# Two layers of a 1024-wide model on one core: gate logits in split form, scores of both directions summed, and token halves behind the second layer's output projection

## The reference, cut to what matters

```python
def gla_chunked(q, k, v, logg):          # one direction; the other one runs on flipped tokens
    b = jnp.cumsum(logg, axis=3)
    qe = q * jnp.exp(b)
    ke = k * jnp.exp(-b)
    a = jnp.where(mask, jnp.einsum('bhncd,bhnjd->bhncj', qe, ke), 0.0)
    o_intra = jnp.einsum('bhncj,bhnjv->bhncv', a, v)
    ...
    o = o_intra + jnp.einsum('bhncd,bhndv->bhncv', qe, s_before)

def gla_mixer(h, w_in, w_gate_up, b_gate, out_g, w_o):
    ...
    logit = jnp.einsum('bsir,ire->bsie', z, w_gate_up.astype(f32)) + b_gate.astype(f32)
    ...
    o = rmsnorm(o_f + o_b, out_g).reshape(B, S, GLA_V)

def second_block(...):
    y = _hybrid_mixer(h, w_in, ..., w_out, cos, sin)         # ends in merged @ w_out
    x = x + g1 * _rmsnorm(y, norm_g[l, 1])
    h = _rmsnorm(x, norm_g[l, 2]) * (1.0 + sc2) + sh2
    y = _conv_ffn(h, w_up, conv_w, conv_b, w_down)
    x = x + g2 * _rmsnorm(y, norm_g[l, 3])
```

## Time and profile before

| what | value |
| --- | --- |
| time, median of 3 runs | 2041.51 us (2040.54 to 2043.55) |
| profiled execution | 2038.21 us, its span 2036.5 us |
| mean granted TensorE clock | 0.989 of full |
| TensorE busy | 1990.7 us, 98% |
| VectorE, ScalarE, GpSimd busy | 1126.3, 745.3, 575.2 us |
| linear attention, heads (us from start) | 765 to 817 |
| layer two, last `w_out` matmul to first feed-forward matmul | 1632.6 to 1655.8 |

### The profile page before, as it was taken

One profiled execution on the slowest core, in us unless ns is written; L12 is line 12 of the kernel. 1 busy time (PEld: TensorE's weight loads), 2 busy tenths in 40 slices (PEclk: granted clock), 3 DMA queues, 4 the chain that ended last, 5 costly groups with the idle time before them and its releaser, 6 DMA issues.

```text
span 2036.5 us, 23938 instructions
## 1 busy us (share of the span) xinstructions
PE 1990.7 (98%) x9414; PEld 1625.2 (80%) x9414; DVE 1126.3 (55%) x1132; ACT 745.3 (37%) x801; POOL 575.2 (28%) x513
## 2 busy tenths in 40 slices
PE   9999999999999999999999999999999979999996
PEld 7766788888877988888888877788888858888885
DVE  6797355555564437455465456773334465545446
ACT  6665332322334523332222234345552343222322
POOL 1101289993000000189993002522310100000000
PEclk9999999999999999999999999999999999999998
DMA  7300144442222220144442213412123312332231
GB/s 227 98 21 1 62 170 151 154 165 97 88 67 103 84 101 23 62 157 155 163 158 92 100 62 130 114 42 84 63 83 110 104 56 84 103 103 102 83 103 42
DMA packets 32781, 202.01 MB, mean 99 GB/s; under 512 B 3872, under 2 KB 4000, under 8 KB 10048
## 3 DMA queue, kind: packets, MB, share of 16 engines
q1 hardware_dynamic: 25984, 168.44, 24.1%
q0 software_dynamic: 6720, 32.51, 5.1%
HBM read 191.50 MB, written 2.10 MB: 95 GB/s over the span
## 4 chain that ended last, share of the span: by engine, by line
PE 93%; DVE 4%; ACT 2%; issue 1%; DMA 0%; SPq 0%; DVEq 0%; ACTq 0%
PE ps L260 26%; PE ps L262 26%; PE ps L261 25%; PE ps L700 2%; PE ps L1609 1%; PE ps L687 1%; PE ps L382 1%; PE ps L290 1%; PE ps L292 1%; PE ps L291 1%; PE ps L1156 1%; PE ps L1593 1%; PE ps L676 1%; PE ps L675 1%; PE ps L1164 1%
## 5 line engine op out<-in xcount | busy, mean ns | idle before, releaser
L222 ACT ACTIVATE w_hi<-w_raw 128x2048 fp32r<-128x2048 f32 x143 | 274.0, 1916 | 676.8 <-PE ps L262 676.6
L230 DVE TENSOR_TENSOR w_lo<-w_raw,w_hi 128x2048 fp32r<-128x2048 f32 x139 | 323.3, 2326 | 158.5 <-ACT w_hi L222 156.9
L260 PE MATMUL ps<-h_hi,w_hi 128*128 128x512 f32 x944 | 380.4, 403 | 10.7 <-DVE h_lo L440 5.4
L262 PE MATMUL ps<-h_hi,w_lo 128*128 128x512 f32 x944 | 372.5, 395 | 0.0
L261 PE MATMUL ps<-h_lo,w_hi 128*128 128x512 f32 x944 | 372.2, 394 | 0.0
L392 POOL TENSOR_TENSOR sq<-sq 128x1024 f32<-128x1024 f32 x11 | 36.4, 3307 | 825.9 <-ACT sq L361 705.9
L1405 POOL TENSOR_SCALAR ada_t<-ada_w,prm 128x256 f32<-128x256 f32 x192 | 220.3, 1147 | 13.3 <-DMA ada_w<-in_ada 12.4
L260 PEld LDWEIGHTS ps<-h_hi,w_hi 128*128 128x128 f32 x944 | 180.0, 191 | 55.1 <-issue 13.6
L262 PEld LDWEIGHTS ps<-h_hi,w_lo 128*128 128x128 f32 x944 | 179.9, 191 | 38.4
L261 PEld LDWEIGHTS ps<-h_lo,w_hi 128*128 128x128 f32 x944 | 180.4, 191 | 36.5 <-issue 1.2
L1013 DVE TENSOR_TENSOR x<-x,ps 128x1024 f32<-128x1024 f32 x128 | 155.8, 1217 | 80.8 <-PE ps L262 80.8
(11 more groups left out here) (312 smaller groups left out, 3211.4 us busy)
## 6 DMA issues: line engine op xcount, KB each, us to landing
w_raw<-in_wb SPq DMA_DIRECT2D x153, 1024.0 KB, 4.9
ada_w<-in_ada POOLq DMA_DIRECT2D x24, 1024.0 KB, 5.3
a_sw<-a_g POOLq DMA_DIRECT2D x20, 128.0 KB, 2.7
x<-in_xT SPq DMA_DIRECT2D x4, 512.0 KB, 7.8
out_T<-x SPq DMA_DIRECT2D x4, 512.0 KB, 2.8
x_rot<-x_g POOLq DMA_DIRECT2D x12, 128.0 KB, 3.0
w_raw<-in_wb SPq DMA_DIRECT2D x4, 256.0 KB, 6.4
b_k<-b_k POOLq DMA_DIRECT2D x4, 256.0 KB, 5.3
```

The costliest lines, as they stand in the source:

```text
L222: act.activation(w_hi[:, slot], w_raw[:, slot], ACT.Copy).then_inc(hi_done, 1)
L230: dve.tensor_tensor(w_lo[:, slot], w_raw[:, slot], w_hi[:, slot].bitcast(F32), ALU.subtract).then_inc(split_done, 1)
L260: pe.matmul(out, w[0], h[0], start=start, stop=False)
L262: return pe.matmul(out, w[1], h[0], start=False, stop=stop)
```

## The change

1. Gate logits. The z block holds z three times (rows 0 to 31, 32 to 63, 64 to 95). `g_z` becomes fp32r over 128 rows: high part, low rest, high part. The gate weights come in a 128-row table (512 KB instead of 128) and are stacked as high, high, low rest. Each head's product is then one fp32r matmul. VectorE gets three instructions (`gate_parts`).
2. Scores. A new VectorE instruction `both_ways` adds the masked scores of both directions, and TensorE multiplies the sum by the values: half the matmuls of line 1156. `sums(h - 1)` moves ahead of the chunk products. The decays of the keys of heads 1 to 3 move from VectorE (2 instructions of 512 columns) to ScalarE (8 of 128 columns); those of head 1 come during the projections.
3. Layer two. The last `w_out` block and both blocks of the first feed-forward unit are done in two token halves of 256 columns; norm, addition, second norm and split run by halves, one half's vector work beside the other's matmuls. `y` isn't cleared any more. The last `w_out` rows are read from PSUM. Squares of `x` are summed by 256-column ones-matmuls, those of half 1 between the tiles of block 1 of half 0.
4. Semaphores of four table loads are joined in one (`tables_in`), norms are renumbered.

```diff
 def logits(d):
     if d == 0:
-        pe.wait_ge(gup_in, 16)
-        pe.wait_ge(g_ev, 1)
+        pe.wait_ge(g_zl, 1)
     ...
-        last = pe.matmul(ps[:, 4 + h, :], gl["g_up"][:, d, h * P:(h + 1) * P], gl["g_z"][:], start=True, stop=True)
+        last = pe.matmul(ps[:, 4 + h, :], gl["g_ups"][:, d, h * P:(h + 1) * P], gl["g_z"][:], start=True, stop=True)
 for h in range(GLA_H):
+    if h >= 1:
+        sums(h - 1)
     pe.wait_ge(g_kc, 2 * h + 2)
     ...
-    if h >= 1:
-        sums(h - 1)
-    pe.wait_ge(g_am, 2 * (h + 1))
+    pe.wait_ge(g_as, h + 1)
     ...
-            for d in range(2):
-                pe.matmul(ps[:, bank + i, t * P:(t + 1) * P], gl["g_v"][:, t, vcol], gl["g_a"][:, d, t, :],
-                          start=t == 0 and d == 0, stop=False)
+            pe.matmul(ps[:, bank + i, t * P:(t + 1) * P], gl["g_v"][:, t, vcol], gl["g_a"][:, 0, t, :],
+                      start=t == 0, stop=False)
```

The parts on VectorE and ScalarE, and layer two on TensorE:

```diff
+def gate_parts():                                   # VectorE, ahead of the projections
+    up, whole = gl["g_ups"], gl["g_up"]
+    dve.wait_ge(gup_in, 16)
+    link(dve, dve.tensor_copy(up[:], whole[:]))
+    dve.tensor_tensor(up[64:96], whole[64:96], up[64:96].bitcast(F32), ALU.subtract)
+    dve.wait_ge(g_ev, 1)
+    dve.tensor_tensor(gl["g_z"][32:64], ps[32:64, 0, :], gl["g_z"][32:64].bitcast(F32), ALU.subtract).then_inc(g_zl, 1)
+def both_ways(h):                                   # VectorE, behind queries(h)
+    dve.wait_ge(g_am, 2 * (h + 1))
+    dve.tensor_tensor(a[:, 0], a[:, 0], a[:, 1], ALU.add).then_inc(g_as, 1)
+def decayed(h):                                     # ScalarE, behind rstd of head h - 2
+    for d in range(2):
+        for n in range(TT):
+            ins = act.activation(gl["g_kd"][:, d, w], qk("g_k", d)[:, h, w], ACT.Copy, scale=...)
+        ins.then_inc(g_kd, 1)
...
+def wout_pe(pe, b0):
+    pe_block(pe, b0, b0 % 2, hh, 3, each=lambda k: pe.wait_ge(t_lo, k // 2 + 1))
+    pe_block(pe, b0 + 1, (b0 + 1) % 2, hh, 1)
+    pe_block(pe, b0 + 2, b0 % 2, hh, 0)
+    pe.wait_ge(split_done, b0 + 4)
+    pe.wait_ge(proj_ev, 10)
+    half(0, b0 + 3, lambda k: None).then_inc(o_part, 1)
+    half(1, b0 + 3, first_sums).then_inc(block_done, 1)      # first_sums: at k == 3, waits o_fold 3 and o_sq 4
+    pe.wait_ge(o_sq, 5)
+    half_sums(1)
 def ffn_pe(pe, b0, n):
-    ffn_up(pe, 0, b0, b0 % 2, rows=56)
+    for j in range(4):
+        renorm_sums(pe, 0, j)
+    ffn_up_half(pe, b0, 0, 0)                                # waits r_lo tile by tile
+    ffn_up_half(pe, b0, 1, 0, each=lambda k: renorm_sums(pe, 1, k - 1) if k in (1, 2, 3, 4) else None)
+    ffn_up_half(pe, b0, 0, 1)
+    ffn_up_half(pe, b0, 1, 1)
...
+def wout_act(act, b0):
+    ...                                                      # squares of y, half 0 of the last rows
+    std(0, o_sum, 1)
+    act.wait_ge(block_done, b0 + 4)
+    act.activation(quarter_slot(1), half_rows(1), ACT.Square).then_inc(o_sq, 1)
+    ...                                                      # four quarters of the next high part between square(0, 0..3)
+    std(1, o_sum, 2)
+    std(0, r_sum, 4)
+    rows(0)
+    for j in range(4):
+        square(1, j)
+    std(1, r_sum, 8)
+    rows(1)
+def wout_dve(dve, b0):
+    ...                                                      # three copies to y, each with the rest of a block
+    added(0)
+    split_lo(dve, b0 + 5, (b0 + 5) % 2)
+    rows(0)
+    added(1)
+    rows(1)
+def wout_pool(pool):                                         # two folds of 1024 columns and one of 512
```

More of the change, by code:

```diff
@@ L1228, in gla_act @@
                     turned(0)
+                    decayed(1)
             act.preload_act_table_set("natural_log_exp_and_others")
@@ L1370, in gla_dve @@
                     queries(h + 1)
+                    both_ways(h + 1)
             root(GLA_H - 1)
@@ new lines, in build, with quarter_slot, renorm_slot, half_sums @@
+        std_count = lambda which, h: 6 + 2 * which + h + 1
+        HALF_BANK = (2, 4)
+        half_rows = lambda h: ps[:, HALF_BANK[h]:HALF_BANK[h] + 2, HALF[h]]
+        def quarter_slot(i):
+            return ff["f_c"][:, i // 2, (i % 2) * S:(i % 2 + 1) * S].rearrange("p (a s) -> p a s", a=2)
+        def renorm_slot(q):
+            return quarter_slot((2, 3, 0, 1)[q % 4])
+        def wout_pe(pe, b0):
+            hh = (mx["x_mhi"], mx["x_mlo"])
+            def half_sums(h):
+                for i in range(2):
+                    last = pe.matmul(ps[:, 6 + h, 0:S // 2], ones[:], quarter_slot(h)[:, i, :], start=False, stop=i == 1)
+                last.then_inc(o_sum, 1)
+            def half(h, b, each):
+                for k in range(KT):
+                    each(k)
+                    for n in range(2):
+                        last = three(pe, ps[:, HALF_BANK[h] + n, HALF[h]], wtile(b % 2, k * 256 + n * P),
+                                     (hh[0][:, k, HALF[h]], hh[1][:, k, HALF[h]]), k == 0, k == KT - 1)
+                return last
+            def first_sums(k):
+                if k == 3:
+                    pe.wait_ge(o_fold, 3)
+                    for h in range(2):
+                        pe.matmul(ps[:, 6 + h, 0:S // 2], ones[:], sq[:, 0, HALF[h]], start=True, stop=False)
+                    pe.wait_ge(o_sq, 4)
+                    half_sums(0)
+            pe_block(pe, b0, b0 % 2, hh, 3, each=lambda k: pe.wait_ge(t_lo, k // 2 + 1))
[7 more added lines that the diff above has]
+            half_sums(1)
@@ new lines, in renorm_sums, with std, square, rows @@
+        def renorm_sums(pe, h, j):
+            pe.wait_ge(r_sq, 4 * h + j + 1)
+            for i in range(2):
+                last = pe.matmul(ps[:, 6 + h, 0:S // 2], ones[:], renorm_slot(4 * h + j)[:, i, :],
+                                 start=j == 0 and i == 0, stop=j == 3 and i == 1)
+            last.then_inc(r_sum, 1)
+        def wout_act(act, b0):
+            def std(h, needed, count):
+                act.wait_ge(needed, count)
+                alink(act, act.activation(rstd[:, HALF[h]], ps[:, 6 + h, 0:S // 2], ACT.Ln, bias=pc("eps"), scale=1.0 / D))
+                act.activation(rstd[:, HALF[h]], rstd[:, HALF[h]], ACT.Exp, scale=-0.5).then_inc(n_std, 1)
+            def square(h, j):
+                q = 4 * h + j
+                act.wait_ge(o_add, q + 1)
+                if q == 3:
+                    act.wait_ge(o_sum, 2)
+                elif q >= 4:
+                    act.wait_ge(r_sum, q - 3)
+                act.activation(renorm_slot(q), x[:, 2 * j:2 * j + 2, HALF[h]], ACT.Square).then_inc(r_sq, 1)
+            def rows(h):
+                for k in range(KT):
+                    act.wait_ge(n_row, 16 + 8 * h + k + 1)
+                    act.activation(h_hi[:, k, HALF[h]], trow[:, k % 4, HALF[h]], ACT.Identity,
+                                   bias=modT[:, 24 + k:25 + k]).then_inc(n_hi, 1)
+            act.wait_ge(n_app, 48)
+            for j in range(2):
+                next_hi(act, b0 + j + 2, (b0 + j) % 2)
+                act.wait_ge(proj_ev, 8 + j + 1)
+                act.activation(two(sq[:, j]), y[:, 2 * j:2 * j + 2, :], ACT.Square).then_inc(o_sq, 1)
+            next_hi(act, b0 + 4, b0 % 2)
+            act.wait_ge(proj_ev, 11)
+            act.wait_ge(o_fold, 1)
+            act.activation(two(sq[:, 1]), y[:, 4:6, :], ACT.Square).then_inc(o_sq, 1)
+            act.wait_ge(o_part, 1)
+            act.activation(quarter_slot(0), half_rows(0), ACT.Square).then_inc(o_sq, 1)
+            std(0, o_sum, 1)
+            act.wait_ge(block_done, b0 + 4)
+            act.activation(quarter_slot(1), half_rows(1), ACT.Square).then_inc(o_sq, 1)
+            b = b0 + 5
+            quarter_hi(act, b, b % 2, 0)
+            square(0, 0)
+            quarter_hi(act, b, b % 2, 1)
+            quarter_hi(act, b, b % 2, 2)
+            square(0, 1)
+            quarter_hi(act, b, b % 2, 3)
+            square(0, 2)
+            square(0, 3)
+            std(1, o_sum, 2)
[5 more added lines that the diff above has]
+            rows(1)
@@ new lines, in ffn_up_half @@
+        def ffn_up_half(pe, b, which, h, each=None):
+            pe.wait_ge(split_done, b + which + 1)
+            for k in range(KT):
+                if which == 0:
+                    pe.wait_ge(r_lo, 8 * h + k + 1)
+                if each is not None:
+                    each(k)
+                for n in range(2):
+                    last = three(pe, ps[:, 2 * which + n, HALF[h]], wtile((b + which) % 2, k * 256 + n * P),
+                                 (h_hi[:, k, HALF[h]], h_lo[:, k, HALF[h]]), k == 0, k == KT - 1)
+            if h == 1:
+                last.then_inc(block_done, 1)
@@ L2570 @@
     i = {k: np.asarray(v) for k, v in inputs.items()}
-    up = zeros(32, 2, S)
-    up[0:16, 0] = i["gla_w_gate_up"][0, 0]
-    up[16:32, 1] = i["gla_w_gate_up"][0, 1]
+    up = zeros(P, 2, S)
+    for r in range(0, 96, 32):
+        up[r:r + 16, 0] = i["gla_w_gate_up"][0, 0]
```

(1 more changed line is left out.)

180 lines of the change are left out of this document (110 added, 70 removed).

## The result

The changed kernel takes 2018.64 us (median of 4 runs, 2015.13 to 2020.76) beside 2042.32 (4 runs, 2040.54 to 2043.55): ratio 0.989 (0.9874 to 0.9905). A second measurement of it, beside eleven runs of the kernel before, gave 0.9903 (0.9887 to 0.9919). Its profiled execution took 2016.82 us, with a span of 2015.0 and a mean granted clock of 0.991. The forecast was 2020.8, within 2016.5 to 2028.

The account below looks back on a forecast made before the run. TensorE, in flight for 98% of the span, was taken as the bound. Gains of 7.4 (logits), 9.0 (heads) and 4.3 (layer two) sum to 20.7 us, taking the median from 2041.5 to 2020.8, range 2016.5 to 2028.

Parts of the forecast that it names:

- Logits: Gate logits: fp32r products save 5.4 us, no clock fall 1.7, small steps between matmul types the rest; 7.4 in all.
- The wait before block 8: TensorE's wait of about 1 us for block 8's rest on VectorE was to shift with its chain and not grow.
- Heads: Linear attention heads: a turn of 11.8 us instead of 14.17 three times, and 1.9 in head 0; gain 9.0 us.
- I charge 0.2: Heads: the first state is ready 0.1 to 0.3 us after TensorE is, so 0.2 us of waiting per turn.
- at most 0.3 ahead of the scores: Sign for the heads: TensorE would stand at most 0.3 us ahead of scores times values.
- The rival of a bound VectorE: Heads: VectorE, done at 12.6 with next scores at 12.65, becomes the bound; 2024 to 2028 us, chance 0.12.
- This works only since the decays of keys left VectorE: Heads: VectorE is just in time only because the key decays, 2 x 0.69 us, moved to ScalarE.
- Layer two: From `w_out` to the third feed-forward block: token halves overlap vector work with matmuls; gain 4.3 us after latency.
- The price of 0.39 for a product of 256 columns: Layer two, VectorE's `added`: a 256-column product was taken as 0.39 us, between 0.33 and 0.48.
- 12 us from the last `w_out` matmul to the first of the feed-forward part: Sign for layer two: the gap between these two matmuls would be 12 us, with sums between them.
- steps 1 and 3: Layer two's rebuilt schedule: half 1 of the last `w_out` block ends at 1635.3; TensorE starts feed-forward at 1644.6.
- Slow clock in the heads: Rival: the clock falls to 1.2 GHz in the heads, costing 40 us; time 2061 us, chance 0.03.

Follow-up runs that it names:

- the double and the padded sets: Kernel before with each fp32 gate-logits product made twice (logits stage 148.91 us against 135.44), or made over 128 rows, the added ones zero (133.13 and 133.11).
- l2_only: Kernel before with layer two's token halves alone, logits and heads as before; 2034.37 us (8 runs), ratio 0.997.
- decays_dve: Changed kernel with the decays of the keys back on VectorE as two instructions of 512 columns; 2019.23 us (4 runs), ratio 0.9894.
- whole_second: Changed kernel with the sums of half 1 at once, then half 1 of block 0, then block 1 whole; layer two took 67.10 us, 3.3 more.

## Why the prediction was right, point by point

- **Logits, 7.4 expected, 7.4 measured**, and nearly with the split that was given: 5.4 by the step of the matmuls, 0.4 by the small step behind each set (0.3 was added for it), 1.6 by the clock (1.7 expected). That the logits bring the fall was a guess from what stood ahead of it, and the double and the padded sets bear it out. That it cost 1.7 and not twice that was the luck of this execution, as `l2_only` shows. The wait before block 8 stayed at 1.1 us and moved with its chain.
- **Heads, 9.0 expected, 8.0 measured.** Head 0 gave 1.8 of its 1.9. A turn came out at 12.09 instead of 11.75. Step for step: `within` 2.66 (2.65), sums 1.72, first chunks 1.31 (1.35), second chunks and wait 1.70 (1.35 + 0.2), scores times values 2.02 (1.8), queries times states 2.68. The step that failed is "I charge 0.2" for the states: the wait itself is 0.36, and the matmuls behind it lose 0.24. Together with small differences of the other terms that makes the turn 0.34 longer, three times. Right was that a wait for the states takes over; wrong the signs to look for, "at most 0.3 ahead of the scores".
- **The rival of a bound VectorE** (2024 to 2028) put its price on work that came 0.05 us before its date. The date was the wrong one: VectorE is done at 12.65, as reckoned, but had 1.2 us of its own idle time behind that date and 0.4 ahead of it, and `decays_dve` spent 1.1 of these without any cost. "This works only since the decays of keys left VectorE" was wrong.
- **Layer two, 4.3 expected, 4.6 measured** in this pair of traces, 5.7 on the average. With the 16.9 us by which this part lies earlier after the change, the steps compare at once: first feed-forward matmul 1644.7 (predicted 1644.6), half 0 of block 1 done 1661.4 (1661.5), half 1 of block 0 done 1667.6 (1667.7), rest of the weights awaited 1.36 (1.3), third block done 1685.8 (1685.7). The price of 0.39 for a product of 256 columns, taken between 0.33 and 0.48, is 0.40 in the chain. The 0.3 taken off for latency was too much. What the sum never says is that the 34.6 us of before from which it starts hold 1.7 us of low clock behind the stand at 1655.84: 1.3 of the 4.6 are the clock and not the overlap that the prediction tells of. One sign was written wrongly: it named 12 us from the last `w_out` matmul to the first of the feed-forward part, where steps 1 and 3 themselves give 9.3, and 9.3 it is.
- **Slow clock in the heads**: 1.00 over the whole turn, so nothing of it.
- **The median.** 2020.8 was forecast, and 2018.64 and 2020.54 were measured. The stages say that the change is worth 7.9 + 8.0 + 5.7 = 21.6 us, with the logits and layer two averaged over the traces. The two series gave 23.7 and 18.8, one on each side of it. That the first median lay 2.2 from the forecast is within that chance and no merit of the sum: the heads gave 1.0 less than the sum, and layer two, on the average, 1.4 more.

## What to carry to other kernels

Small products on few rows can be dearer than they look: here they pulled TensorE's clock down for the matmuls that followed, and filling the operand up to all rows, even with zeros, avoided it in both traces. When an engine seems just in time, look for the next date at which somebody truly waits for it, and count its idle time up to there, before paying to unload it. Filling one hole of TensorE with work from ahead of another opens the other; splitting that work in two can close both. An edit that closes a long stand of TensorE also spares the low clock behind it; count the two apart, as cheap matmuls in the stand may bring the second alone. And compare stages at marks, not whole times, where the clock moves the time by more than the edit.

## What the runs showed of the hardware that I had not expected

- The granted clock fell in or behind 3.6 us of fp32 matmuls on 32 rows with TensorE in flight all the time (three of six places), and did not behind 3.4 us of the same matmuls on 128 rows filled up with zeros (four places).
- An fp32 product of four heads took 3.62 us on 32 rows and 3.43 on 128, and the fp32r matmul behind it 0.43 and 0.23.
- A stand of 0.4 us was followed by 0.24 us of loss in the 16 matmuls behind it (2.02 against 1.78; 3.81 against 3.57 in the kernel before), and one of 0.7 us by 0.18 in the 12 chunk products (2.86 against 2.68).
- The gap of 2.8 us before the first feed-forward matmul went with the lower clock in all seven traces that have it open, and so did the second one of `whole_second`; with matmuls of ones in the gap it stayed at 1.00.
- In layer two by whole tiles, the stands of 5.8 and 3.9 us went with a low clock at both places in all six traces; behind the second it cost 1.6 to 2.8 us.
- A stage that no edit touches moved in length by 4.4 us between executions (803.7 to 808.1), with the granted clock in it. The Trainium skill, TensorE: Matmul & The Clock Gate, section What's actually happening, calls the window of the clock gate free-running and its effect different from run to run; the traces agree, with falls that come or stay away and leave 1.7 or 3.4 us of work missing. What decides in one execution, no run here shows.
